# Identity products as plain matmuls instead of transposes, in the norm spreads of a two-block kernel

## The reference

```python
def rms_norm(x, g):                     # over the last axis
    x32 = x.astype(jnp.float32)
    y = x32 * lax.rsqrt(jnp.mean(x32 * x32, axis=-1, keepdims=True) + EPS)
    return (y * g.astype(jnp.float32)).astype(x.dtype)

# first block
xn = rms_norm(h, g_mix_pre); z = xn @ w_in
mix = concat([conformer_conv(..), forgetting_attention(..), short_conv(..), pool(..)]) @ w_out
h = h + rms_norm(mix, g_mix_post)
ff = square(relu(rms_norm(h, g_mlp_pre) @ w_up)) @ w_down
h = h + rms_norm(ff, g_mlp_post)
gate = sigmoid(rms_norm(h, g_ple_pre) @ w_ple_gate)
h = h + rms_norm((p @ w_ple_proj) * gate, g_ple_post)
# second block
z = rmsnorm(x, ln_mix_g) @ w_in         # qa, ka, va, qb, kb, vb, rb, gk_lr, ga, gb
qa = rmsnorm(qa per head of 64, q_norm_g); ka = rmsnorm(ka per head of 64, k_norm_g)
ya = sliding_window_sink_attention(qa, ka, va, sinks)
yb = rmsnorm(gla_chunked(qb, kb, vb, gk), gla_norm_g) * silu(rb)
x = x + (sigmoid(ga) * (ya @ w_branch_a) + sigmoid(gb) * (yb @ w_branch_b)) @ w_out
a, u = split(rmsnorm(x, ln_ffn_g) @ w_ffn_in)
x = x + (silu(causal_dwconv(a)) * u) @ w_ffn_out
```

## Time and profile before

| | |
|---|---|
| time, median of 3 runs | 1510.62 us (1510.5 to 1511.38) |
| the profiled execution | time 1511.38 us, span 1509.6 us |
| mean granted TensorE clock | 0.992 of full speed |
| TensorE busy | 1455.1 us, 96% of the span |
| VectorE, ScalarE, GpSimd busy | 818.1, 571.0, 257.7 us |
| DMA | 129.18 MB, mean 86 GB/s |

### The profile page before, as it was taken

One profiled execution on the slowest core, in us unless ns is written; L12 is line 12 of the kernel. 1 busy time (PEld: TensorE's weight loads), 2 busy tenths in 40 slices (PEclk: granted clock), 3 DMA queues, 4 the chain that ended last, 5 costly groups with the idle time before them and its releaser, 6 DMA issues.

```text
span 1509.6 us, 17723 instructions
## 1 busy us (share of the span) xinstructions
PE 1455.1 (96%) x6972; PEld 1187.7 (79%) x6972; DVE 818.1 (54%) x1150; ACT 571.0 (38%) x836; POOL 257.7 (17%) x169
## 2 busy tenths in 40 slices
PE   7999999999999999889999999999999999999998
PEld 6776768888888887766789877788887888888887
DVE  4598566433333347674767753634444665534554
ACT  4344534522323224443364565422224443323310
POOL 4144244300101013340034202200003000000000
PEclk9999999999999999998999999999999999999999
DMA  6221222332333332211211111232332233232331
GB/s 225 70 71 56 70 71 84 98 100 96 98 98 98 98 98 74 81 56 56 71 56 52 34 56 43 89 107 86 100 106 86 70 112 103 93 111 85 98 98 70
DMA packets 35987, 129.18 MB, mean 86 GB/s; under 512 B 4008, under 2 KB 4136, under 8 KB 35904
## 3 DMA queue, kind: packets, MB, share of 16 engines
q1 hardware_dynamic: 35904, 128.04, 27.4%
HBM read 125.91 MB, written 2.10 MB: 85 GB/s over the span
## 4 chain that ended last, share of the span: by engine, by line
PE 84%; DVE 7%; ACT 3%; POOL 3%; issue 2%; DMA 0%; SPq 0%; POOLq 0%; DVEq 0%; ACTq 0%
PE P L1013 24%; PE P L1015 24%; PE P L1014 24%; PE P L1244 2%; PE P L1034 1%; PE P L1035 1%; PE P L1036 1%; DVE P L1785 1%; POOL AC L2262 1%; ACT WH L1324 1%; DVE WL L1630 1%; POOL H L2271 1%; POOL DD L2262 0%; PE P L1227 0%; PE P L1130 0%
## 5 line engine op out<-in xcount | busy, mean ns | idle before, releaser
L1013 PE MATMUL P<-AH,WH 128*128 128x512 f32 x1104 | 445.3, 403 | 25.8 <-DVE AL L1635 12.5
L1015 PE MATMUL P<-AH,WL 128*128 128x512 f32 x1104 | 433.8, 393 | 0.0
L1014 PE MATMUL P<-AL,WH 128*128 128x512 f32 x1104 | 433.6, 393 | 0.0
L1324 ACT ACTIVATE WH<-WR 128x1024 fp32r<-128x1024 f32 x233 | 245.0, 1052 | 335.1 <-PE P L1015 323.3
L1630 DVE TENSOR_TENSOR WL<-WR,WH 128x1024 fp32r<-128x1024 f32 x216 | 273.0, 1264 | 169.7 <-ACT WH L1324 169.3
L1013 PEld LDWEIGHTS P<-AH,WH 128*128 128x128 f32 x1104 | 209.6, 190 | 77.3 <-issue 27.0
L1015 PEld LDWEIGHTS P<-AH,WL 128*128 128x128 f32 x1104 | 209.4, 190 | 44.8
L1014 PEld LDWEIGHTS P<-AL,WH 128*128 128x128 f32 x1104 | 209.9, 190 | 41.9 <-issue 0.7
L1013 PE MATMUL P<-FH,WH 128*128 128x512 f32 x432 | 168.0, 389 | 0.0
L1014 PE MATMUL P<-FL,WH 128*128 128x512 f32 x432 | 168.0, 389 | 0.0
L1015 PE MATMUL P<-FH,WL 128*128 128x512 f32 x432 | 168.0, 389 | 0.0
(11 more groups left out here) (301 smaller groups left out, 1858.2 us busy)
## 6 DMA issues: line engine op xcount, KB each, us to landing
WR<-in_ws SPq DMA_DIRECT2D x233, 512.0 KB, 3.6
out<-Y SPq DMA_DIRECT2D x8, 256.0 KB, 2.0
H<-in_xT SPq DMA_DIRECT2D x3, 512.0 KB, 8.6
C<-in_const SPq DMA_DIRECT2D x1, 946.5 KB, 11.0
H<-in_xT SPq DMA_DIRECT2D x2, 256.0 KB, 4.6
PR<-in_pT SPq DMA_DIRECT2D x1, 512.0 KB, 4.5
PM<-in_params SPq DMA_DIRECT2D x1, 121.5 KB, 2.9
GKU<-in_gku SPq DMA_DIRECT2D x1, 32.0 KB, 10.5
```

Of the source, the lines that this page charges most:

```text
L1013: e.matmul(P, wh, xh, start=start, stop=False)
L1014: e.matmul(P, wh, xl, start=False, stop=False)
L1015: ins = e.matmul(P, wl, xh, start=False, stop=stop)
L1324: e.activation(m.WH[:, c % NW, :], m.WR[:, c % NRAW, :], ACT.Copy).then_inc(*at.up("w_hi", "w_hi", c))
```

## The change

Two helpers call `matmul` with `start=True, stop=True` instead of `transpose`, with the same operands. The table `NR` gets 32 more columns, and the sinks and decays move to its new end. Other transposes (lines 1119, 1174, 1214 and 1262) stay.

```diff
-        self.NR = f("NR", [128, 416])
+        self.NR = f("NR", [128, 448])
...
-            assert self.nrcol <= 392
+            assert self.nrcol <= 424
...
     def spread_to(P, r):
         for n in range(4):
-            ins = e.transpose(P[:, 128 * n:128 * n + 128], r[:, n:n + 1].broadcast_to([128, 128]), ident)
+            ins = e.matmul(P[:, 128 * n:128 * n + 128], r[:, n:n + 1].broadcast_to([128, 128]), ident,
+                           start=True, stop=True)
         return ins
...
         for n in range(4):
             s = slice(128 * n, 128 * n + 128)
-            ins = e.transpose(m.bank[t.bank][:, s], m.RX[:, j, s], ident)
+            ins = e.matmul(m.bank[t.bank][:, s], m.RX[:, j, s], ident, start=True, stop=True)
         ins.then_inc(*at.up("full", "full", t.id))
...
-        e.activation(m.NR[:, 400:416], halves(flat(m.BC), 128)[:, :, 127], ACT.Exp, scale=1.0 / 16).then_inc(
+        e.activation(m.NR[:, 432:448], halves(flat(m.BC), 128)[:, :, 127], ACT.Exp, scale=1.0 / 16).then_inc(
...
-        e.tensor_scalar(m.NR[:, 392:400], m.p("sinks", 0, 8), -1.0, None, ALU.mult).then_inc(
+        e.tensor_scalar(m.NR[:, 424:432], m.p("sinks", 0, 8), -1.0, None, ALU.mult).then_inc(
...
-        sink = m.NR[:, 392 + 2 * j:394 + 2 * j]
+        sink = m.NR[:, 424 + 2 * j:426 + 2 * j]
...
-                e.scalar_tensor_tensor(m.ST2[:, n, s], m.ST2[:, n - 1, s], m.NR[:, 400 + 4 * hh + n:401 + 4 * hh + n], ps,
+                e.scalar_tensor_tensor(m.ST2[:, n, s], m.ST2[:, n - 1, s], m.NR[:, 432 + 4 * hh + n:433 + 4 * hh + n], ps,
```

## The result

The changed kernel takes 1534.39 us (median of 4 runs, 1531.97 to 1538.89) beside 1511.0 us for the kernel before (4 runs, 1510.5 to 1518.31). The ratio (of the means) is 1.0147, with a 95% interval of 1.0107 to 1.0186: slower by some 22 us (the medians are 23.4 apart), where 8.7 us were forecast and the range ended at 1522.5. The profiled execution took 1535.01 us, with a span of 1533.2, 23.6 more than before.

A forecast was written before the change was run, and what follows sets the result against it. TensorE, busy for 96% of the span, was taken to bound the kernel. Eighteen groups at 0.45 us plus one at 0.6 add 8.7 us to 1510.6: 1519.3 us, range 1515.3 to 1522.5.

The forecast's parts named there:

- Two instructions a call, and 0.80 us a group: Both helpers: each float32 matmul call makes two instructions (x104, x8, x40); a group takes 0.80 us instead of 0.35.
- The sum of the groups: All 19 changed groups: 18 at 0.45 us and one at 0.6 add 8.7 us.
- the 0.6 for it: Post-norm group of the first mixer, at half clock: +0.6 us, between +0.45 and +0.86.
- The chain through the five norm groups: The five qk_norm groups: all are links of the chain, so each one's 0.45 us counts.
- "I cover nothing", for the group norm: Group norm's four spreads: no slack at 945.69, so the later 1.23 us gap absorbs none of their 1.8 us.
- The rival of swallowed idle time: Idle stretches behind norm groups and group norm's spreads absorb 4.05 us, leaving 4.65: 1515.3 us; chance 0.07.
- The wider table, "I take 0, with nothing on either side": Tiles behind NR move by 128 bytes: no instruction changes shape or count, so cost 0, without a range.
- The signs: Group step 0.80 us, norm groups some 4 us later, last spread some 8, 1.23 us gap kept, idle near 54.5.
- the steeper price: Changed groups: two passes per instruction, each at a transpose's cost, make a group 1.40 us: 1530.6 us; chance 0.04.
- The clock gave nothing back: Five half-clock stretches: matmuls keep the clock at 2.4 GHz, returning at most 12.0 us: 1507.3 us; chance 0.02.
- The collision rival: VectorE's 3.96 us operation at 853.89 goes ahead of GpSimd's, returning some 3.8 us: 1515.5 us; chance 0.02.

The follow-up runs named there:

- the run with 352 columns: The changed kernel with NR at 352 columns instead of 448, tiles behind it 256 bytes below their place in the kernel before: 1522.89 us, ratio 1.0057.

## Why the prediction was wrong, by its steps

*Two instructions a call, and 0.80 us a group*: right. x104, x40 and x8, and 0.81 us. The `diag_mm` group was the right row.

*The sum of the groups*: right in size, 8.4 us against 8.7. The group of p1 took 0.99 us; the low clock was not there in that execution, so that the 0.6 for it became 0.14. What a group costs at half clock stands in the run with 352 columns, where that of p3 fell into such a stretch: 1.87 us.

*The chain through the five norm groups*: right. All are links of it, the first and the last 9.40 us apart where they were 7.53, by about four times 0.46:

```profile
743.33 1.16 PE P L1196 x8
...
752.73 0.91 PE P L1196 x8
```

*"I cover nothing", for the group norm*: wrong. I took the product of VectorE at 945.69 for the one that waits for the last spread. But each of the four spreads serves two products, and this is the fifth of the eight, so it used the third spread. The seventh, the first that needs the last spread, came 8.8 us after that spread's start at 945.27:

```profile
954.04 0.74 DVE L2106 SCALAR_TENSOR_TENSOR G<-G,PM,P 128x512 f32<-128x512 f32 x1
```

The last group had slack. In the trace after, TensorE starts its last spread at 962.71, while VectorE and GpSimd are still at the products of the third:

```profile
961.71 0.74 DVE L2107 SCALAR_TENSOR_TENSOR G<-G,PM,P 128x512 f32<-128x512 f32 x1
962.53 1.66 POOL L2387 TENSOR_TENSOR G<-G,RS 128x512 f32<-128x512 f32 x1 [1.82 <-DVE G L2107]
962.71 1.05 PE L1092 MATMUL P<-C,NR 128*128 128x128 f32 x8
962.97 0.74 DVE L2107 SCALAR_TENSOR_TENSOR G<-G,PM,P 128x512 f32<-128x512 f32 x1
```

The gap of 1.23 us at 952.57 is gone in all three kernels with the matmuls, and there in those with transposes (1.20 with only the wider table). It takes 1.2 of the 8.4 us back. The rival of swallowed idle time was thus true for a part of its place, and false for the norm groups.

*The wider table, "I take 0, with nothing on either side"*: this is the step that failed. It was worth more than the change of instruction. The price that I said no row gives was 0.020 us a triple, for 678 triples: 13.6 us worked out so, 12.5 us summed over the steps in the trace after. I had argued by what instructions the edit adds, and an address adds none. The range could not reach it, since this term had been given no width.

*The signs*: the counts, the 0.80 a group and the idle time near 54.5 (56.1) came out as named. The starts did not: the norm groups began 13.7 us later, not 4, and the last spread 19.7 us later, not 8; and the gap of 1.23 us did not stay. The two late starts pointed to a loss outside the edited groups.

*The rivals*: the steeper price named 1530.6, near the measured time, by a mechanism that did not happen: the group takes 0.81, not 1.40 us. Had I only seen the time, I would have taken it as confirmed. The clock gave nothing back: five stretches of half clock became three, and their sum stayed at 23.9 us. Over a stretch of equal length around the start of the second mixer it was lower than before, first before and then after:

```profile
700.00:730.00 30.00, 27.20 (x120) 21.43 (x119) 18.82 (x26) 13.74 (x15) 1.90 (x1) 0.83 0.12 36
```
```profile
705.00:735.00 30.00, 27.93 (x102) 19.59 (x101) 13.11 (x13) 11.58 (x12) 0.00 (x0) 0.72 0.12 36
```

As it stands in the same stretch at 0.72 with only the wider table too, and the stretches of low clock at 66 and 216 us are missing in the changed kernel, this share of the clock is not put down to the matmuls. Where such stretches fall was not settled.

*The collision rival* came true in the other direction, and elsewhere. A scan of VectorE took 1.21 us before and 3.43 after, as GpSimd's weight split started 0.03 us ahead of it:

```profile
72.17 2.40 POOL L2253 TENSOR_TENSOR WL<-WR,WH 128x1024 fp32r<-128x1024 f32 x1 [0.54 <-ACT WH L1325]
72.20 3.43 DVE L1727 TENSOR_TENSOR_SCAN FX<-FX 4x512 f32<-4x512 f32 x1
```

It leads to a gap of 2.01 us before 86.10 that wasn't there before:

```profile
86.10 0.70 PE L1111 MATMUL P<-KAUG,QAUG 66*128 66x256 f32 x2 [2.01 <-DVE SB L1739]
```

The matmuls are not needed for it: the run with only the wider table has it too (3.43 us for the same scan). With only the matmuls the scan started 0.01 us ahead and took 1.21, and the split took 3.40; the gap was 1.77 us. In the run with the weights moved, as in the kernel before, the two did not meet. Before, TensorE was at half clock from 65.9 to 69.3, which made that split start later. In the executions without this slow stretch the two meet. That the slow stretch decides it is argued from these traces and was not tested.

The account of the profiled executions, step by step of TensorE's stream: groups 8.4, triples behind `NR` at full clock 12.5, idle time 1.6 (2.0 and 1.0 us of waits behind the scan, 1.2 swallowed, small rest), steps in which one of the two was at half clock 0.6, all other steps 0.5, together 23.6 us.

## What to carry to other kernels

An edit that resizes a small buffer ahead of others moves them all. Before such an edit is costed at nothing, compare the start addresses of TensorE's moving tiles and weight tiles modulo 256 before and after: here 128 bytes of padding cost more than the 76 added matmuls. This was seen for float32r matmuls of 512 columns in an unbroken stream, and not for those of 256. The sign in the profile is a longer mean (389 to 395 ns) in groups whose line was not touched, for some tiles and not for others. Compare times at equal granted clock where they differ by little. When a total agrees with a rival, look for the rival's own row before believing it.

## What the runs showed of the hardware that was not expected

- Float32r matmuls of 512 columns started every 0.2267 us when the streamed tile and the weight tiles started at the same address modulo 256, and every 0.233 us at the other multiples of 32 (0.229 to 0.230 at 64, 0.234 at 160). The 0.233 is 2.9% more. Matmuls of 256 columns, with `AH` or `AL` as the weights, kept their 0.12 us wherever `AH` was put.
- With only the low weights out of line, two of three matmuls paid: the one that used them and the one during which they were loaded.
- The kernel before was 1.4 us longer for each 0.001 less of mean granted clock, over 20 runs with clocks of 0.987 to 0.994.
- Four 128x128 float32 products took 0.81 us as eight matmul instructions, against 0.35 us as four transposes: a factor of 2.3. Where the Trainium skill states a factor of four for FP32 ("TensorE: Matmul & The Clock Gate", table of terms), no group in these runs showed it.
